# Scaling, transposing and splitting the state-space heads' output ahead of its projection, in another order

## The chip, the cores and the metric

The kernel runs on one core of a Trainium2 chip. The metric is the device time of one execution in microseconds (us). Each version was run several times; the median counts.

## What is computed

The reference is a chain of three transformer-like blocks on 256 tokens of width 1024. The change lies in the third, at the end of its state-space mixer. The 32 heads give y, 256 x 2048 values. With the gate z and eight groups of 256 columns:

```
y = y * silu(z)
y = y * rsqrt(mean(y^2 over each group of 256) + 1e-6) * norm_g
y_ssd = y @ w_ssd_o                    # 2048 x 1024
mixed = sigmoid(g_attn) * y_attn + sigmoid(g_ssd) * y_ssd
x = x + mixed @ w_out
```

All products are in f32 accuracy: the kernel makes one f32 product of three faster ones, from "upper" and "lower" halves of both operands (upper: the value rounded to fp32r, lower: the rest), as high x high + high x low + low x high.

## The kernel before

**Layout.** The 256 tokens are two tiles of 128 partitions (t = 0, 1; NT = 2). Every matrix product reads its weights from a stream of slots of 128 x 1024 values (512 KB), loaded by SyncE (L1530) into a ring of four buffers. A slot whose product is "split" gets its halves on the way: ScalarE copies the upper half to `wpair` (L477), and VectorE subtracts it from the raw slot for the lower one (L480). `wpair` has three places. The order of all this is written out by hand for each engine; there is no planner. The class Splitter keeps a counter of slots: `split.to(o)` splits all slots below o, `split.step()` the next one, `split.cover(stage)` all of a stage and up to two more. Both engines run through their own list in strict order, so a split stands exactly where it is written. Three counting semaphores tie it together: `w_hi` (upper half written), `w_lo` (lower half written; TensorE's `weights()` and SyncE's reload wait for it) and `w_used` (TensorE has used a slot up; ScalarE waits for slot o - 3 before it writes slot o). TensorE raises `w_used` with the first matmul or transpose behind the slot (`hold`, `release`).

**The stages here.** "gssd" (8 slots) is the product for the state-space gate g_ssd, "ssdo" (16 slots; slot k holds rows 128k to 128k + 127 of w_ssd_o) the projection of y, "wo3" the one by w_out. `ssdo_at` is the number of ssdo's first slot. The gate's first four slots give its lower 512 columns, before the heads; the last four ("gate pieces", L1858) lie beside the heads, two at their start and two behind them.

**The heads.** For each head TensorE sums rows (L1883, L1884), ScalarE takes exponentials (L2245, L2246), VectorE masks (L2895), and TensorE multiplies with x (L1897 to L1900). After each four heads VectorE adds (L2903) and multiplies with silu(z) (L2911), and ScalarE squares the group with a sum (L2236). At the end of the heads these run out one by one.

**Behind the heads, before the change.** VectorE splits one more slot, makes the mean squares (L2916, raises `y_ms`), ScalarE takes the square root (L2257; a load of its function table stands ahead of it), VectorE the reciprocal (L2919). Then VectorE scales y in four blocks of 512 columns: for both t a product with the reciprocal root (L2926), a wait, for both t a product with the row norm_g (L2930), a wait, and `y_normed` goes up by one (L2934). All four blocks are scaled before VectorE goes on. TensorE transposes y in eight groups of two 128-column blocks and both t (`y_group`, four transposes each, L1913), group i and i + 1 after block i / 2, into two PSUM banks in turn (6 and 7). ScalarE copies each group's upper half to `xpair` (L2272, raises `y_hi`), VectorE writes the lower half (L2941, raises `tr_out`). `xpair` holds four groups. TensorE waits with a bank for its lower half, two groups back. Groups 0 to 3 come ahead of ssdo's first product; groups 4 to 7 after slots 1, 3, 5 and 7. Group i serves slots 2i and 2i + 1. ssdo's result lies in banks 0 to 3. ScalarE and VectorE split up to slot 3 (`ssdo_at + 4`) ahead of their half of group 4, up to slot 5 ahead of group 5, and so on, and the rest behind group 7. ScalarE takes the two sigmoids of the gate (lower columns L2262, upper columns from the banks 0 and 1 L2265) ahead of its copies. On POOL, the load of the keys of a later stage (L1620) waits for the first `y_normed`. At the end VectorE gates the result and adds (L2949, L2952) and `mix3` is transposed for wo3 (L664).

Group 0 to 3 on TensorE, the last two lines being the order of the splits on ScalarE:

```
for i in range(4):
    y_group(i)
...
if k % 2 == 1 and k < 8:
    y_group(4 + k // 2)
...
if i >= 4:
    split.to(ssdo_at + 2 * (i - 4) + 4)
```

Of the kernel before, what the change touches and what calls it, by code (L numbers as in the profile page):

```python
# [27 lines left out]
ACT = mybir.ActivationFunctionType  # L28
AX = mybir.AxisListType

P = 128
# [353 lines left out]
def build(nc, wstream, rows, mixrow, cols, diag, consts, relb, keys, x_tok, xT_in, memT_in, ws, out, tbuf):  # L385
    ctx = ExitStack()
    with ctx:
# [5 lines left out]
        def S(name):  # L393

            if name not in sems:
                sems[name] = ctx.enter_context(nc.semaphore(name))
            return sems[name]
# [42 lines left out]
        def wait_lin(eng, g):  # L440

            if g > 0:
                for t in range(NT):
                    eng.wait_ge(S(f"lin_out{t}"), g)
# [74 lines left out]
        def bank(g, t):  # L519

            return psum[:, 2 * (g % 2) + t, :]
# [543 lines left out]
        def row_of(name):  # L1065
            return par[:, ROW[name] % 2, :]
# [360 lines left out]
        def y_pair(i, a):  # L1427

            return xpair[:, a, 2 * (i % 4):2 * (i % 4) + 2, :]

        def y_bank(i):
            return psum[:, 6 + (Q["y3"] + i) % 2, :].rearrange("p (c s) -> p c s", c=2)

        ssdo_at = ORDER[STAGES["ssdo"].slot][1]

# [199 lines left out]
        def _(pe):  # L1635
# [268 lines left out]

            def y_group(i):
                q = Q["y3"] + i
                if i % 2 == 0:
                    pe.wait_ge(S("y_normed"), i // 2 + 1)
                if q >= 2:
                    pe.wait_ge(S(f"tr_out{q % 2}"), q // 2)  # L1910
                for j in range(4):
                    c = 2 * i + j // 2
                    mm = pe.transpose(psum[:, 6 + q % 2, j * P:(j + 1) * P], y3[:, j % 2, c * P:(c + 1) * P], ident)  # L1913
                    if j == 0:
                        release(mm)
                mm.then_inc(S("tr_done"), 1)

            for i in range(4):
                y_group(i)
            s = STAGES["ssdo"]  # L1920
            wait_lin(pe, s.tile)
            for k in range(16):
                if k % 2 == 0:
                    q = Q["y3"] + k // 2
                    pe.wait_ge(S(f"tr_out{q % 2}"), q // 2 + 1)
                if k >= 14:
                    continue
                w = weights(pe, s.slot + k)
                for nn in range(2):
                    for t in range(NT):  # L1930
                        products(pe, bank(s.tile + nn, t), [xpair[:, a, k % 8, tt(t)] for a in (0, 1)],
                                 part(w, halves(nn)), k == 0, False)
                hold(s.slot + k)
                if k % 2 == 1 and k < 8:
                    y_group(4 + k // 2)
            w = [weights(pe, s.slot + k) for k in (14, 15)]
            for nn in range(2):
                for t in range(NT):
# [57 lines left out]
        def _(act):  # L1996
# [243 lines left out]
            for h in range(SSD_H):  # L2240
                act.wait_ge(S("rowsum"), h + 1)
                if h >= 4:
                    act.wait_ge(S("ydone"), h - 3)
                b = psum[:, 4 + h % 2, :]
                act.activation(ebuf[:, h % 4, 0:256], b[:, 0:256], ACT.Exp, bias=tiny[:, 12, h:h + 1])  # L2245
                act.activation(ebuf[:, h % 4, 256:384], b[:, 256:384], ACT.Exp, bias=tiny[:, 12, 32 + h:33 + h])\  # L2246
                   .then_inc(S("sexp"), 1)
                if h in (6, 7):
                    split.step()
                if h >= 10 and h % 4 in (2, 3):  # L2250
                    squares((h - 10) // 4, h % 4 - 2)
            for g in range((SSD_H - 10) // 4 + 1, SSD_G):
                for t in range(NT):
                    squares(g, t)
            split.step()
            act.wait_ge(S("y_ms"), 1)
            act.activation(grs, gst, ACT.Sqrt).then_inc(S("y_sd"), 1)  # L2257
            s = STAGES["gssd"]
            split.cover("gssd")
            act.wait_ge(S("lin_out0"), s.tile + 1)  # L2260
            act.wait_ge(S("lin_out1"), s.tile + 1)
            act.activation(g3[:, :, 0:HALF], g3[:, :, 0:HALF], ACT.Sigmoid).then_inc(S("gate3_low"), 1)  # L2262
            for t in range(NT):
                act.wait_ge(S(f"lin_done{t}"), s.tile + 2)
                act.activation(g3[:, t, HALF:D], bank(s.tile, t), ACT.Sigmoid).then_inc(S(f"lin_out{t}"), 1)  # L2265
            for i in range(8):
                if i >= 4:
                    split.to(ssdo_at + 2 * (i - 4) + 4)
                act.wait_ge(S("tr_done"), Q["y3"] + i + 1)
                if i >= 4:  # L2270
                    act.wait_ge(S("w_used"), ssdo_at + 2 * (i - 4) + 2)
                copy(y_pair(i, 0), y_bank(i)).then_inc(S("y_hi"), 1)  # L2272
            split.cover("ssdo", more=1)
            split.begin("wo3")
            act_x(act, "mix3")
# [62 lines left out]
        def _(dve):  # L2338
# [550 lines left out]
            for i in range(SSD_H + 5):  # L2889
# [16 lines left out]
                if h >= 0 and h % 4 == 3:  # L2906
                    g = h // 4
                    dve.wait_ge(S("yout"), g + 1)
                    for t in range(NT):
                        yg = y3[:, t, g * 256:(g + 1) * 256]  # L2910
                        dve.tensor_tensor(yg, yg, zz(t, g // 2)[:, g % 2 * 256:(g % 2 + 1) * 256], ALU.mult)\  # L2911
                           .then_inc(S("y_gated"), 1)
            split.step()

            dve.wait_ge(S("y_sq"), NT * SSD_G)
            chain(dve.tensor_scalar(gst, gst, 1.0 / 256, RMS_EPS, ALU.mult, ALU.add))  # L2916
            dve.nop().then_inc(S("y_ms"), 1)
            dve.wait_ge(S("y_sd"), 1)
            chain(dve.reciprocal(gst, grs))  # L2919
            wait_row(dve, "ssdn")  # L2920
            gate_end = ORDER[STAGES["gssd"].slot + STAGES["gssd"].nslot - 1][1] + 1
            for b in range(4):
                c = slice(b * HALF, (b + 1) * HALF)
                for t in range(NT):
                    yt = y3[:, t, c].rearrange("p (g d) -> p g d", g=2)
                    chain.mark(dve.tensor_tensor(yt, yt, gst[:, 8 * t + 2 * b:8 * t + 2 * b + 2].unsqueeze(2)  # L2926
                                                 .to_broadcast([P, 2, 256]), ALU.mult))
                chain.wait()
                for t in range(NT):
                    chain.mark(dve.tensor_tensor(y3[:, t, c], y3[:, t, c], row_of("ssdn")[:, c], ALU.mult))  # L2930
                    if split.at < gate_end:
                        split.step()
                chain.wait()
                dve.nop().then_inc(S("y_normed"), 1)  # L2934
            dve.nop().then_inc(S("row_used"), 1)
            split.cover("gssd")
            for i in range(8):
                if i >= 4:
                    split.to(ssdo_at + 2 * (i - 4) + 4)
                dve.wait_ge(S("y_hi"), i + 1)  # L2940
                dve.tensor_tensor(y_pair(i, 1), y_bank(i), y_pair(i, 0).bitcast(F32), ALU.subtract)\  # L2941
                   .then_inc(S(f"tr_out{(Q['y3'] + i) % 2}"), 1)
            split.cover("ssdo", more=1)
            s = STAGES["ssdo"]
            for n in range(2):
                for t in range(NT):
# [188 lines left out]
```

## Time and profile before

| what | value |
|---|---|
| time, median of 3 runs | 3109.84 us |
| lowest and highest | 3109.38, 3110.26 us |
| span of the profiled execution | 3107.9 us |
| the profiled execution's own time | not given apart from its span |
| mean granted clock of TensorE | 0.982 |
| busy TensorE / VectorE / ScalarE | 96% / 64% / 44% |
| instructions | 52456 |

The span runs from the first to the last instruction of one execution. A line such as L2941 is a line of the kernel. "Busy" of TensorE is the share of the span in which a matmul ran, by modelled ends. "Granted clock" is the share of 2.4 GHz that the chip lets TensorE have; its two levels are 1.00 (2.4 GHz) and 0.50 (1.2 GHz), and a mean over a stretch lies between them. A row of the timeline merges neighbours of the same kind: start in us, length in us from the start of the first to the end of the last, what, and in brackets the idle time of the engine before it, with what ended it.

### The profile page before, as it was taken

The page shows a single profiled execution, that of the slowest core. Times are in us where ns is not written, and L with a number is a line of the kernel's source. Part 1 is how long each engine was busy: PE and PEld are TensorE (multiplying, and loading weights), DVE is VectorE, ACT ScalarE, POOL GpSimd, SP SyncE. Part 2 cuts the span into 40 slices and gives each one's busy share as a digit, 9 for nine tenths or more (in the row PEclk, how much of TensorE's full clock was granted, in tenths as well). Part 3 has the DMA queues.
Part 4 walks back from the last instruction along what each step waited for, and adds up shares of the span by engine and source line. Part 5 has one row for each costly group of instructions (what it writes and reads, how often), then busy time and mean ns, then how long its engine had stood idle before and what let it go on. Part 6 is the DMA issues. An engine that isn't in the chain of part 4 may idle for free. (4 is left out here: it accounts for less than half of the span.)

```text
span 3107.9 us, 52456 instructions
## 1 busy us (share of the span) xinstructions
PE 2983.3 (96%) x19012; PEld 2654.8 (85%) x19012; DVE 1984.8 (64%) x3483; ACT 1362.0 (44%) x2015; POOL 197.6 (6%) x207
## 2 busy tenths in 40 slices
PE   8999998998999999999999999998898899999999
PEld 8987767997999699998799776997797888888888
DVE  5565565556557655556755664686599866666666
ACT  4333433434344334435343543565446744433333
POOL 0000000000000000000000000010057700000000
PEclk9999999999999999999999999999999999999999
DMA  7564253555554555555355543443442255555554
GB/s 275 188 216 150 102 176 129 190 187 202 184 185 154 189 188 183 185 187 183 131 199 186 186 156 118 163 143 103 142 157 89 69 188 189 184 187 179 179 183 159
DMA packets 140575, 523.73 MB, mean 169 GB/s; under 512 B 15698, under 2 KB 15698, under 8 KB 137616
## 3 DMA queue, kind: packets, MB, share of 16 engines
q1 hardware_dynamic: 135072, 490.79, 47.1%
q0 software_dynamic: 4784, 29.94, 2.6%
q8 instruction: 95, 1.56, 0.2%
q10 hardware_dynamic: 576, 1.05, 0.1%
q14 instruction: 48, 0.39, 0.0%
HBM read 520.65 MB, written 1.06 MB: 168 GB/s over the span
## 5 line engine op out<-in xcount | busy, mean ns | idle before, releaser
L480 DVE TENSOR_TENSOR wpair<-ring,wpair 128x1024 fp32r<-128x1024 f32 (+1 forms) x862 | 1044.5, 1220 | 740.2 <-ACT wpair L477 736.1
L509 PE MATMUL psum<-xpair,wpair 128*128 128x256 f32 x11712 | 1476.5, 285 | 21.3 <-DVE wpair L480 14.5
L509 PEld LDWEIGHTS psum<-xpair,wpair 128*128 128x128 f32 x11712 | 1444.5, 193 | 59.4 <-DVE wpair L480 35.1
L477 ACT CAST wpair<-ring 128x1024 fp32r<-128x1024 f32 (+1 forms) x888 | 919.0, 1044 | 815.5 <-PE psum L509 737.6
L509 PE MATMUL psum<-wpair,hpair 128*128 128x512 f32 x3120 | 751.6, 392 | 5.0 <-DVE hpair L942 5.0
L509 PEld LDWEIGHTS psum<-wpair,hpair 128*128 128x128 f32 x3120 | 572.7, 189 | 117.4 <-issue 7.5
L509 PE MATMUL psum<-wpair,xpair 128*128 128x512 f32 (+3 forms) x1728 | 403.2, 391 | 4.1 <-DVE wpair L480 1.8
L509 PEld LDWEIGHTS psum<-wpair,xpair 128*128 128x128 f32 x1728 | 321.9, 193 | 73.2 <-issue 7.2
L917 ACT ACTIVATE small<-psum 128x256 f32<-128x256 f32 x132 | 50.7, 384 | 230.9 <-PE psum L509 230.9
L953 ACT ACTIVATE small<-psum 128x256 f32<-128x256 f32 x92 | 35.4, 384 | 259.9 <-PE psum L509 259.9
L931 DVE TENSOR_TENSOR small<-small,psum 128x256 f32<-128x256 f32 x132 | 55.6, 421 | 136.7 <-ACT small L917 136.7
L1574 POOL DMA_DIRECT2D arena<-rows x18 | 9.6, 535 | 1533.3 <-DVEq L1127 1186.1
L942 DVE TENSOR_TENSOR hpair<-small,hpair 128x256 fp32r<-128x256 f32 x236 | 100.4, 426 | 8.1
L1984 PE MATMUL psum<-hpair,small 128*128 128x128 f32 x512 | 70.5, 281 | 12.3 <-ACT hpair L2317 10.2
L1984 PEld LDWEIGHTS psum<-hpair,small 128*128 128x128 f32 x512 | 63.2, 193 | 17.1 <-DVE small L3077 14.7
L3077 DVE TENSOR_SCALAR small<-kc,small 128x128 f32<-128x128 f32 x256 | 76.5, 341 | 0.1
L940 DVE CAST hpair<-small 128x256 fp32r<-128x256 f32 x236 | 69.4, 294 | 8.1
L480 POOL TENSOR_TENSOR wpair<-ring,wpair 128x1024 fp32r<-128x1024 f32 x26 | 62.5, 2409 | 163.5 <-DVE wpair L480 147.7
L722 ACT CAST xpair<-psum 128x512 fp32r<-128x512 f32 x60 | 34.2, 587 | 65.9 <-PE psum L664 39.7
L1005 DVE TENSOR_TENSOR small<-small,arena 128x256 f32<-128x256 f32 x92 | 60.9, 662 | 0.1
L1309 ACT ACTIVATE arena<-arena,st 128x128 f32<-128x128 f32 (+1 forms) x64 | 28.6, 447 | 73.8 <-DVE st L1339 73.8
L1230 DVE SCALAR_TENSOR_TENSOR arena<-arena,pcol 128x256 f32<-128x256 f32 x144 | 58.9, 480 | 1.1 <-DVE arena L2674 0.5
(344 smaller groups left out, 1813.3 us busy)
## 6 DMA issues: line engine op xcount, KB each, us to landing
ring<-wstream SPq DMA_DIRECT2D x934, 512.0 KB, 3.3
arena<-rows POOLq DMA_DIRECT2D x18, 1024.0 KB, 5.3
arena<-diag POOLq DMA_DIRECT2D x2, 1728.0 KB, 10.6
arena<-tbuf POOLq DMA_DIRECT2D x2, 1024.0 KB, 9.3
arena<-x_feat ACTq DMA_DIRECT2D x4, 256.0 KB, 7.4
res<-x_tok POOLq DMA_DIRECT2D x1, 1024.0 KB, 8.4
gb<-mem_feat POOLq DMA_DIRECT2D x1, 1024.0 KB, 17.4
arena<-keys POOLq DMA_DIRECT2D x1, 1024.0 KB, 5.2
```

What stands on the lines that cost most here:

```text
L477: eng.copy(hi, raw).then_inc(S("w_hi"), 1)
L480: eng.tensor_tensor(wpair[:, 1, o % PAIRS, 0:w], raw, hi.bitcast(F32), ALU.subtract)\
L509: mm = pe.matmul(out_, a[i], b[j], start=start and n == 0, stop=stop_ and last)
L917: act.activation(gated(f0 + f), psum[:, 4 + (f0 + f) % 2, 0:SEQ], ACT.Silu).then_inc(S("hid_act"), 1)
L931: dve.tensor_tensor(whole(h), gated(h), psum[:, 4 + h % 2, SEQ:2 * SEQ], ALU.mult)\
L940: dve.tensor_copy(hpair[:, 0, h % 2, :], src).then_inc(S("hid_hi"), 1)
L942: dve.tensor_tensor(hpair[:, 1, h % 2, :], src, hpair[:, 0, h % 2, :].bitcast(F32), ALU.subtract)\
L953: act.activation(gated(f), psum[:, 4 + f % 2, 0:SEQ], ACT.Gelu).then_inc(S("hid_act"), 1)
L1005: dve.tensor_tensor(whole(h), gated(f), weight(f + step * i), ALU.mult).then_inc(S("hid_whole"), 1)
L1230: chain.mark(eng.scalar_tensor_tensor(out=acc[:, f, :], in0=src, scalar=w, in1=acc[:, f, :], op0=ALU.mult, op1=ALU.add))
L1984: mm = pe.matmul(psum[:, n % 4, j * P:(j + 1) * P], oh1[:, n % 2, j, :], oh2[:, n % 2, j, :].bitcast(F32), start=True, stop=True)
L3077: ins = dve.tensor_scalar(oh1[:, n % 2, j, :], iota, selT[:, 0, tok], selT[:, 2, tok], ALU.is_equal, ALU.mult)
```

## The change

It touches only the end of the heads. Scalings go by groups of 256 columns in one fused pass for each t, and every pass raises `y_normed`. VectorE's list interleaves the scalings with splits and lower halves. Transposes use four banks (4 to 7) in turn; groups 0 and 1 come ahead of ssdo's slot 0, groups 2 and 3 behind it, and groups 4 to 7 behind slots 3, 5, 7 and 9. Slot 0 does the upper 512 columns first, so that it waits for the gate's banks later. ScalarE loads the table of the root ahead of the last squares and that of the sigmoid behind the root, and has the upper and lower gate sigmoids between and behind the first copies.

```diff
--- before.py
+++ after.py
@@ -1429,7 +1429,7 @@
             return xpair[:, a, 2 * (i % 4):2 * (i % 4) + 2, :]
 
         def y_bank(i):
-            return psum[:, 6 + (Q["y3"] + i) % 2, :].rearrange("p (c s) -> p c s", c=2)
+            return psum[:, 4 + i % 4, :].rearrange("p (c s) -> p c s", c=2)
 
         ssdo_at = ORDER[STAGES["ssdo"].slot][1]
 
@@ -1904,21 +1904,19 @@
 
             def y_group(i):
                 q = Q["y3"] + i
-                if i % 2 == 0:
-                    pe.wait_ge(S("y_normed"), i // 2 + 1)
-                if q >= 2:
-                    pe.wait_ge(S(f"tr_out{q % 2}"), q // 2)
+                pe.wait_ge(S("y_normed"), NT * (i + 1))
+                if i >= 4:
+                    pe.wait_ge(S(f"tr_out{q % 2}"), q // 2 - 1)
                 for j in range(4):
                     c = 2 * i + j // 2
-                    mm = pe.transpose(psum[:, 6 + q % 2, j * P:(j + 1) * P], y3[:, j % 2, c * P:(c + 1) * P], ident)
+                    mm = pe.transpose(psum[:, 4 + i % 4, j * P:(j + 1) * P], y3[:, j % 2, c * P:(c + 1) * P], ident)
                     if j == 0:
                         release(mm)
                 mm.then_inc(S("tr_done"), 1)
 
-            for i in range(4):
-                y_group(i)
+            y_group(0)
+            y_group(1)
             s = STAGES["ssdo"]
-            wait_lin(pe, s.tile)
             for k in range(16):
                 if k % 2 == 0:
                     q = Q["y3"] + k // 2
@@ -1926,13 +1924,18 @@
                 if k >= 14:
                     continue
                 w = weights(pe, s.slot + k)
-                for nn in range(2):
+                for nn in (1, 0) if k == 0 else (0, 1):
+                    if k == 0 and nn == 0:
+                        wait_lin(pe, s.tile)
                     for t in range(NT):
                         products(pe, bank(s.tile + nn, t), [xpair[:, a, k % 8, tt(t)] for a in (0, 1)],
                                  part(w, halves(nn)), k == 0, False)
                 hold(s.slot + k)
-                if k % 2 == 1 and k < 8:
-                    y_group(4 + k // 2)
+                if k == 0:
+                    y_group(2)
+                    y_group(3)
+                elif k % 2 == 1 and 3 <= k <= 9:
+                    y_group(4 + (k - 3) // 2)
             w = [weights(pe, s.slot + k) for k in (14, 15)]
             for nn in range(2):
                 for t in range(NT):
@@ -2249,27 +2252,39 @@
                     split.step()
                 if h >= 10 and h % 4 in (2, 3):
                     squares((h - 10) // 4, h % 4 - 2)
+            act.activation(spare, eps_col, ACT.Sqrt)
             for g in range((SSD_H - 10) // 4 + 1, SSD_G):
                 for t in range(NT):
                     squares(g, t)
-            split.step()
             act.wait_ge(S("y_ms"), 1)
             act.activation(grs, gst, ACT.Sqrt).then_inc(S("y_sd"), 1)
-            s = STAGES["gssd"]
-            split.cover("gssd")
-            act.wait_ge(S("lin_out0"), s.tile + 1)
-            act.wait_ge(S("lin_out1"), s.tile + 1)
-            act.activation(g3[:, :, 0:HALF], g3[:, :, 0:HALF], ACT.Sigmoid).then_inc(S("gate3_low"), 1)
-            for t in range(NT):
-                act.wait_ge(S(f"lin_done{t}"), s.tile + 2)
-                act.activation(g3[:, t, HALF:D], bank(s.tile, t), ACT.Sigmoid).then_inc(S(f"lin_out{t}"), 1)
-            for i in range(8):
-                if i >= 4:
-                    split.to(ssdo_at + 2 * (i - 4) + 4)
+            split.to(ssdo_at + 1)
+            act.activation(spare, eps_col, ACT.Sigmoid)
+            split.to(ssdo_at + 2)
+
+            def y_upper(i):
+
                 act.wait_ge(S("tr_done"), Q["y3"] + i + 1)
                 if i >= 4:
                     act.wait_ge(S("w_used"), ssdo_at + 2 * (i - 4) + 2)
                 copy(y_pair(i, 0), y_bank(i)).then_inc(S("y_hi"), 1)
+
+            s = STAGES["gssd"]
+            for t in range(NT):
+                act.wait_ge(S(f"lin_done{t}"), s.tile + 2)
+            y_upper(0)
+            y_upper(1)
+            for t in range(NT):
+                act.activation(g3[:, t, HALF:D], bank(s.tile, t), ACT.Sigmoid).then_inc(S(f"lin_out{t}"), 1)
+            split.to(ssdo_at + 3)
+            y_upper(2)
+            y_upper(3)
+            act.wait_ge(S("lin_out0"), s.tile + 1)
+            act.wait_ge(S("lin_out1"), s.tile + 1)
+            act.activation(g3[:, :, 0:HALF], g3[:, :, 0:HALF], ACT.Sigmoid).then_inc(S("gate3_low"), 1)
+            for i in range(4, 8):
+                split.to(ssdo_at + 2 * (i - 4) + 4)
+                y_upper(i)
             split.cover("ssdo", more=1)
             split.begin("wo3")
             act_x(act, "mix3")
@@ -2910,37 +2925,46 @@
                         yg = y3[:, t, g * 256:(g + 1) * 256]
                         dve.tensor_tensor(yg, yg, zz(t, g // 2)[:, g % 2 * 256:(g % 2 + 1) * 256], ALU.mult)\
                            .then_inc(S("y_gated"), 1)
-            split.step()
-
             dve.wait_ge(S("y_sq"), NT * SSD_G)
-            chain(dve.tensor_scalar(gst, gst, 1.0 / 256, RMS_EPS, ALU.mult, ALU.add))
-            dve.nop().then_inc(S("y_ms"), 1)
+            dve.tensor_scalar(gst, gst, 1.0 / 256, RMS_EPS, ALU.mult, ALU.add).then_inc(S("y_ms"), 1)
+            wait_row(dve, "ssdn")
             dve.wait_ge(S("y_sd"), 1)
             chain(dve.reciprocal(gst, grs))
-            wait_row(dve, "ssdn")
-            gate_end = ORDER[STAGES["gssd"].slot + STAGES["gssd"].nslot - 1][1] + 1
-            for b in range(4):
-                c = slice(b * HALF, (b + 1) * HALF)
+
+            def y_norm(g):
+
                 for t in range(NT):
-                    yt = y3[:, t, c].rearrange("p (g d) -> p g d", g=2)
-                    chain.mark(dve.tensor_tensor(yt, yt, gst[:, 8 * t + 2 * b:8 * t + 2 * b + 2].unsqueeze(2)
-                                                 .to_broadcast([P, 2, 256]), ALU.mult))
-                chain.wait()
-                for t in range(NT):
-                    chain.mark(dve.tensor_tensor(y3[:, t, c], y3[:, t, c], row_of("ssdn")[:, c], ALU.mult))
-                    if split.at < gate_end:
-                        split.step()
-                chain.wait()
-                dve.nop().then_inc(S("y_normed"), 1)
-            dve.nop().then_inc(S("row_used"), 1)
-            split.cover("gssd")
-            for i in range(8):
-                if i >= 4:
-                    split.to(ssdo_at + 2 * (i - 4) + 4)
+                    yg = y3[:, t, g * 256:(g + 1) * 256]
+                    dve.scalar_tensor_tensor(out=yg, in0=yg, scalar=gst[:, 8 * t + g:8 * t + g + 1],
+                                             in1=row_of("ssdn")[:, g * 256:(g + 1) * 256], op0=ALU.mult,
+                                             op1=ALU.mult).then_inc(S("y_normed"), 1)
+
+            def y_lower(i):
+
                 dve.wait_ge(S("y_hi"), i + 1)
                 dve.tensor_tensor(y_pair(i, 1), y_bank(i), y_pair(i, 0).bitcast(F32), ALU.subtract)\
                    .then_inc(S(f"tr_out{(Q['y3'] + i) % 2}"), 1)
+
+            y_norm(0)
+            y_norm(1)
+            split.to(ssdo_at + 1)
+            y_norm(2)
+            y_lower(0)
+            y_lower(1)
+            split.to(ssdo_at + 2)
+            y_norm(3)
+            split.to(ssdo_at + 3)
+            y_lower(2)
+            y_lower(3)
+            for g in range(4, SSD_G):
+                y_norm(g)
+            dve.wait_ge(S("y_normed"), NT * SSD_G)
+            dve.nop().then_inc(S("row_used"), 1)
+            for i in range(4, 8):
+                split.to(ssdo_at + 2 * (i - 4) + 4)
+                y_lower(i)
             split.cover("ssdo", more=1)
+            dve.wait_ge(S("gate3_low"), 1)
             s = STAGES["ssdo"]
             for n in range(2):
                 for t in range(NT):
```

## Rows read from the trace of the kernel before

**Rows 1.** The page: its first line.
```profile
span 3107.9 us, 52456 instructions
```

**Rows 2.** The chain that ended last, 2125 to 2200: start, length, what.
```profile
2132.78 1.31 DVE arena L2930 x2
...
2134.32 1.23 DVE wpair L480
```

**Rows 3.** TensorE's timeline, 2117 to 2200 us.
```profile
2117.91 5.73 PE L509 MATMUL psum<-wpair,xpair 128*128 128x512 f32 x24
2125.88 1.09 PE L1913 MATMUL psum<-kc,arena 128*128 128x128 f32 x8 [2.24 <-DVEq L2934]
2136.29 1.94 PE L1913 MATMUL psum<-kc,arena 128*128 128x128 f32 x8 [9.32 <-DVE xpair L2941]
2137.88 7.27 PE L509 MATMUL psum<-wpair,xpair 128*128 128x512 f32 x24
2144.99 0.60 PE L1913 MATMUL psum<-kc,arena 128*128 128x128 f32 x4
2145.35 5.74 PE L509 MATMUL psum<-wpair,xpair 128*128 128x512 f32 x24
...
2163.12 22.39 PE L509 MATMUL psum<-wpair,xpair 128*128 128x512 f32 x96
```

**Rows 4.** The timeline of all engines at the end of the heads, 2116 to 2127 us.
```profile
2116.71 0.21 ACT L2236 ACTIVATION_READ_ACCUMULATOR arena<-arena 128x1 f32 x1
...
2117.53 0.42 ACT L2236 ACTIVATE arena<-arena 128x256 f32<-128x256 f32 x1 [0.60 <-DVE arena L2911]
...
2118.86 0.76 DVE L2911 TENSOR_TENSOR arena<-arena 128x256 f32<-128x256 f32 x2
2119.32 0.42 ACT L2236 ACTIVATE arena<-arena 128x256 f32<-128x256 f32 x1 [0.88 <-DVE arena L2911]
...
2120.04 0.19 ACT L2236 ACTIVATION_READ_ACCUMULATOR arena<-arena 128x1 f32 x1
...
2121.19 1.28 ACT L2257 ACT_TABLE_LOAD   x1
...
2122.34 0.17 DVE L2916 TENSOR_SCALAR st<-st 128x16 f32<-128x16 f32 x1
...
2122.60 0.22 ACT L2257 ACTIVATE st<-st 128x16 f32<-128x16 f32 x1
...
2122.85 0.25 DVE L2919 RECIPROCAL st<-st 128x16 f32<-128x16 f32 x1 [0.34 <-ACT st L2257]
2123.14 1.29 DVE L2926 TENSOR_TENSOR arena<-arena,st 128x512 f32<-128x512 f32 x2
...
2126.04 1.06 ACT L2265 ACTIVATE arena<-psum 128x512 f32<-128x512 f32 x2
2126.12 0.64 POOL L1620 DMA_DIRECT2D arena<-keys  x1 [71.68 <-DVEq L2934]
```

**Rows 5.** VectorE's timeline, in the convolution before the heads.
```profile
2069.19 1.67 DVE L2870 SCALAR_TENSOR_TENSOR arena<-arena,pcol 128x256 f32<-128x256 f32 x4
```

**Rows 6.** The timeline of ScalarE and VectorE behind the transposes of group 4.
```profile
2145.63 0.59 ACT L2272 CAST xpair<-psum 128x512 fp32r<-128x512 f32 x1 [1.83 <-PE psum L1913]
2146.11 1.05 ACT L477 CAST wpair<-ring 128x1024 fp32r<-128x1024 f32 x1
...
2147.19 1.23 DVE L480 TENSOR_TENSOR wpair<-ring,wpair 128x1024 fp32r<-128x1024 f32 x1 [0.26 <-ACT wpair L477]
```

**Rows 7.** TensorE's timeline elsewhere: behind idle times of 1.39, 0.61 and 2.27 us.
```profile
1068.91 5.98 PE L509 MATMUL psum<-xpair,wpair 128*128 128x256 f32 x48 [1.39 <-DVE wpair L480]
...
2258.61 3.14 PE L509 MATMUL psum<-xpair,wpair 128*128 128x256 f32 x24 [0.61 <-DVE wpair L480]
...
2274.44 4.58 PE L509 MATMUL psum<-xpair,wpair 128*128 128x256 f32 x24 [2.27 <-DVE wpair L480]
```

**Rows 8.** Windows: stretch, its us, busy time (instructions) of each engine, clock, DMA, GB/s.
```profile
2274.00:2277.00 3.00, 2.56 (x12) 2.56 (x13) 2.96 (x17) 1.53 (x2) 2.52 (x2) 0.55 0.47 147
```

## The prediction

> **What bounds the kernel now.** I first read the page and then three views of the stretch between the last state-space head and the output product ("ssdo"). TensorE carries the kernel, so this change can move the time only where TensorE stands still. [Rows 1] give the span against which the sum is made. In the chain of waits, look for which engine holds the chain while TensorE is idle: it is VectorE, with the last of the scalings (L2926, L2930) and one split of weights (L480) [rows 2]. TensorE's own timeline shows the two gaps: 2.24 us before the first eight transposes, and 9.32 us before the next eight, which VectorE's first lower halves (L2941) end [rows 3]. The first product of ssdo starts at 2137.88. TensorE had finished the gate pieces at 2117.91 + 5.73 = 2123.64. So 14.2 us lie between them, of which 3 are transposes. From 2137.88 on TensorE is hardly ever idle until 2185.51 (2163.12 + 22.39), and all splits run in its shadow. Two prices follow. One slot is 12 matmuls: 22.39 less a tail of 0.15, over 8, is 2.78 us. One group of transposes adds 2145.35 - 2144.99 = 0.36 us [rows 3]. I first ask what starts the products earlier, then whether the shadow behind them still holds.
>
> **Before the first product.**
> (1) The wait for the root. The last square ends at 2120.23; the split of slot 0 and a table load of 1.28 us stand between it and the root [rows 4]. After the change the table comes ahead of the squares: ScalarE is free at 2116.92, load and a small activation of 0.2 us last to 2118.4, two squares of group 6 to 2119.25, and group 7 is ready at 2119.32 as before. The 0.60 us and 0.88 us that ScalarE idled there [rows 4] hide the load; without them it would cost up to 1.28. VectorE's split before the mean square also goes. Mean square at 2120.3 (0.17), root (0.22), reciprocal (0.25), with small gaps: the first scaling starts at 2121.05 in place of 2123.14.
> (2) The scalings. Sixteen passes of 512 at about 0.65 (two in 1.29, [rows 4]) become sixteen fused ones of 256. Not seen in this form; the nearest row is the convolution's, four of 128x256 in 1.67 with one of them about 0.48, so 0.40 us apart [rows 5]. Bounds are 0.34 (two plain products of that size take 0.75, [rows 4]) and 0.50. Groups 0 and 1 end at 2122.7, the split of slot 0 (1.14 apart) at 2123.8, group 2 at 2124.6.
> (3) The transposes. Group 0 starts when the gate pieces end, 2123.64, and is out 0.60 later, 2124.25. ScalarE after the root: slot 0 (1.0), load of the sigmoid table (1.28), small activation (0.2), slot 1 (1.0), so also 2124.25. Upper half 0.59, lower half 0.69, 0.13 to TensorE: **the first product starts at 2125.7, which is 12.2 us earlier.** Only 1.0 us of idle time is left.
> At this place a rule speaks against the change. The table loads here last 1.28 us and the next instruction starts right behind (2121.19 + 1.28 = 2122.47, and the root, which also waits for VectorE, runs at 2122.60) [rows 4]. The Trainium skill, "ScalarE: Activation LUTs", section "What ACT_TABLE_LOAD costs", adds a drain of about 1380 ns, 2.66 us a switch; the loads' gaps in this trace do not show it. What it would do is a rival below.
> (4) Clock. The first 24 matmuls of ssdo take 7.27 us, the next 24 take 5.74 [rows 3]: they started at 1.2 GHz after the 9.32 us gap. With a gap of 1.0 this goes: **-1.5 us**.
> (5) Groups 2 and 3 of the transposes now stand behind slot 0: two times 0.36, **+0.7 us**. The upper gate's sigmoid (two in 1.06, [rows 4]) ends at 2126.3, before the second half of slot 0 needs its banks at 2127.1: nothing. The lower gate's sigmoid (1.06) comes in ScalarE's wait for group 4: nothing; its reader on VectorE comes at the end of ssdo. The load of the keys on POOL's queue starts at some 2121.5 in place of 2126.12 [rows 4], runs 1 MB beside SP's loads, and nobody waits for it before the next stage but one. SP's loads follow VectorE's splits: that for slot 4 is issued at 2123.9 in place of 2122.6 and wanted after 2138: nothing.
> (6) VectorE's queue. In order: low 0 and 1 to 2126.1, split 1 to 2127.2, group 3 to 2128.0, split 2 to 2129.2, low 2 and 3 from 2129.7 (they wait for group 2 and 3, transposed at 2128.5) to 2130.9, groups 4 to 7 (8 times 0.40) to 2134.2, and only then split 3, to 2135.6. TensorE wants slot 3 at 2134.8. **+0.9 us**, from 0.4 to 1.7 by the bounds in (2). If this is late it is the only early stop.
>
> **Behind the first product.** Here the cover is lost. Group i of the last four is now transposed after slots 3, 5, 7, 9, but the splits are still written as "to slot 4 for group 4, to 6 for group 5, ..." on ScalarE and VectorE, each ahead of that group's halves. When TensorE reaches slot 4, ScalarE has cast slots 0 to 3 and stands in its wait for group 4, which TensorE has only just transposed. The cast of slot 4 is queued behind the copy of group 4, VectorE's split behind its lower half. The same holds for slots 6, 8 and 10. Before the change group 4 came after slot 1 with slots 2 and 3 already split, so 5.6 us of products hid this chain. Its length stands in one round of the trace: transposes start at 2144.99, copy at 2145.63, cast at 2146.11, VectorE's split from 2147.19 to 2148.42 [rows 6]. With 0.13 to TensorE that is 3.56 us after the start of the group, where TensorE would have gone on after 0.36: 3.2 us a stop. The bounds are 2.8 and 3.7. **Four stops, +12.8 us.**
> Sum so far: -12.2 - 1.5 + 0.7 + 0.9 + 12.8 = **+0.7 us**.
> (7) Clock at the stops. TensorE will be idle for some 3.0 us four times. Rows of before bound what that costs. After 1.39 us of idle time 48 matmuls took 5.98, or 24 in 2.99: nothing. After 2.27 us 24 of the same shape took 4.58, against 3.14 a little earlier: 1.4 us [rows 7], and the granted clock of those 3 us was 0.55 [rows 8]. After 9.32 us: 1.5 on products and 0.85 on transposes (1.94 against 1.09, [rows 3]), some 2. The 2.27 us row is the nearest. I take 1.3 a stop, a little less, since the clock may fall while TensorE still waits: **+5.2 us**, from 0 to 8.
> Behind ssdo the same steps follow in the same order, later by the shift: 0, plus or minus 1.5, since the low stretches there can fall otherwise.
> Total +5.9 us on a profiled span of 3107.9, so a span of 3113.8. The runs' median stands 1.9 above that span, and the shift is the same: 3109.84 + 5.9 = **3115.7 us**. A measurement of this kernel can tell about 0.2%, 6.2 us, from no change. The forecast is thus no change that can be told, at the slow edge: 12 us won and given back.
>
> **Rivals.**
> A, slower by more than 0.2%. The place is the first products behind each of the four stops. The forecast's clock price is 1.3 a stop; from (6.2 - 0.7) / 4 = 1.37 on the change counts as slower. For it: the stops are longer than the 2.27 us gap that cost 1.4, and the long gap cost about 2. Against: one low stretch may begin within the stop. At 2.0 a stop: 0.7 + 8.0 = +8.7, 3118.5 us. Chance 0.38.
> B, the clock doesn't fall, as after 1.39 us of idle time [rows 7]: +0.7, 3110.5 us. Against it stands the 2.27 us row. 0.08.
> C, faster: the stops don't occur, the splits being ahead after all, or being much shorter than 3.2. Then -12.1, 3097.7 us. For it: in before, casts do run two slots ahead. Against: the order of the queues, as written. 0.05.
> D, a table switch costs ScalarE more than its row. With 1.4 us more on each of the two moved loads the last square ends 1.1 later and the first upper half 2.4 later; TensorE ends 2.4 later: +8.3, 3118.1 us. Against: no gap behind a load in [rows 4]. 0.05. The rule of "ScalarE: Activation LUTs" named above would be this case.
> The forecast has the rest, 0.44.
>
> **How the numbers follow.** Within 0.2%: forecast and B, 0.52. Slower: A and D, 0.43. Faster: C, 0.05. The range leaves out C and the upper part of A and D: 3110 to 3119 us.
>
> **What would show it.** In the changed profile: first product of ssdo near 2125.7 with under 1.5 us idle before it; its first 24 matmuls without the 7.27; four idle times of TensorE of about 3.0 us, released by VectorE's split (L480), each behind four transposes, at slots 4, 6, 8 and 10; ScalarE waiting some 6 to 7 us for TensorE's transposes each time; granted clock under 1.00 behind the stops; last product of ssdo at about 2191 in place of 2185.5. The forecast is wrong if TensorE runs through at slot 4, or if the stops are there and the granted clock stays at 1.00.

## The result, and the profile after

The changed kernel takes 3118.79 us in the median of six runs (3112.62 to 3126.03), the kernel before 3110.05 us beside it (six runs, 3109.22 to 3117.47). The ratio is 1.0022 with a 95% interval from 1.0011 to 1.0032: slower by about 0.2%, which is where the prediction drew its line. It lies inside the range (3110 to 3119 us). The profiled execution took 3116.99 us with a span of 3115.1 us, 7.2 us longer than before.

TensorE's timeline of the changed kernel, from the last two gate pieces to the transposes of mix3 (start, length, what, and in brackets the idle time before it and what ended it), answers to [rows 3]:

```profile
2118.32 5.74 PE L509 MATMUL psum<-wpair,xpair 128*128 128x512 f32 x24
2123.90 1.03 PE L1912 MATMUL psum<-kc,arena 128*128 128x128 f32 x8
2125.97 3.03 PE L509 MATMUL psum<-wpair,xpair 128*128 128x512 f32 x12 [1.04 <-DVE xpair L2945]
2128.84 1.04 PE L1912 MATMUL psum<-kc,arena 128*128 128x128 f32 x8
2129.63 5.73 PE L509 MATMUL psum<-wpair,xpair 128*128 128x512 f32 x24
2135.97 3.02 PE L509 MATMUL psum<-wpair,xpair 128*128 128x512 f32 x12 [0.61 <-DVE wpair L480]
2138.84 0.60 PE L1912 MATMUL psum<-kc,arena 128*128 128x128 f32 x4
2142.41 8.50 PE L509 MATMUL psum<-wpair,xpair 128*128 128x512 f32 x24 [2.97 <-DVE wpair L480]
2150.74 0.60 PE L1912 MATMUL psum<-kc,arena 128*128 128x128 f32 x4
2154.31 7.35 PE L509 MATMUL psum<-wpair,xpair 128*128 128x512 f32 x24 [2.97 <-DVE wpair L480]
2161.50 0.60 PE L1912 MATMUL psum<-kc,arena 128*128 128x128 f32 x4
2165.07 7.31 PE L509 MATMUL psum<-wpair,xpair 128*128 128x512 f32 x24 [2.97 <-DVE wpair L480]
2172.22 0.60 PE L1912 MATMUL psum<-kc,arena 128*128 128x128 f32 x4
2175.79 18.48 PE L509 MATMUL psum<-wpair,xpair 128*128 128x512 f32 x72 [2.97 <-DVE wpair L480]
2194.30 1.09 PE L664 MATMUL psum<-kc,arena 128*128 128x128 f32 x8
```

Read it in two halves. The 9.32 us of idle time of [rows 3] has become 1.04, and the first product starts at 2125.97. Then four idle times of 2.97 us have appeared, each behind four transposes and each ended by VectorE's split of weights; and behind three of them 24 matmuls take 7.3 to 8.5 us that took 5.74 elsewhere, behind the fourth 72 take 18.48. ScalarE and VectorE at the first of the four, from the timeline of all engines, answer to [rows 6]:

```profile
2139.47 0.58 ACT L2270 CAST xpair<-psum 128x512 fp32r<-128x512 f32 x1 [7.03 <-PE psum L1912]
2139.95 1.99 ACT L477 CAST wpair<-ring 128x1024 fp32r<-128x1024 f32 x2
2140.09 0.69 DVE L2945 TENSOR_TENSOR xpair<-psum,xpair 128x512 fp32r<-128x512 f32 x1 [4.17 <-ACT xpair L2270]
2141.03 2.36 DVE L480 TENSOR_TENSOR wpair<-ring,wpair 128x1024 fp32r<-128x1024 f32 x2 [0.26 <-ACT wpair L477]
```

ScalarE waited 7.03 us for TensorE's transposes, doing nothing, and only then could cast the weights that TensorE wanted at once. At the other three stops it waited 9.43, 8.28 and 8.24 us. The windows of the changed kernel (stretch, its us, busy time and instructions of PE, PEld, DVE, ACT, POOL, granted clock, DMA share, GB/s) show the clock behind the first two stops:

```profile
2136.00:2140.00 4.00, 3.44 (x16) 2.64 (x16) 0.00 (x0) 0.53 (x2) 0.00 (x0) 1.00 0.43 133
2140.00:2144.00 4.00, 1.59 (x4) 1.34 (x5) 3.05 (x3) 1.95 (x3) 0.00 (x0) 0.70 0.16 34
2144.00:2148.00 4.00, 4.00 (x11) 3.14 (x10) 0.00 (x0) 0.00 (x0) 0.00 (x0) 0.50 0.73 235
2148.00:2152.00 4.00, 3.34 (x16) 2.52 (x14) 0.01 (x1) 0.62 (x2) 0.00 (x0) 0.95 0.00 0
...
2156.00:2160.00 4.00, 4.00 (x14) 3.19 (x13) 0.00 (x0) 0.00 (x0) 0.00 (x0) 0.67 0.68 223
```

From 2144 to 2148 eleven matmuls ran at 0.50, that is 1.2 GHz.

Since the start of this stretch moves from run to run for reasons that lie upstream (last section), the experiments are compared by a measure of their own, **the stretch**: from the start of the last gate pieces to the start of mix3's transposes (L664). It is 2185.55 - 2117.91 = 67.6 us before the change and 2194.30 - 2118.32 = 76.0 with it, so 8.3 us more. The distance from the gate pieces to the first product of ssdo is 19.97 us before the change and 7.65 us with it.

### The profile page after: what moved, and what is told of

Same layout as the page of the kernel before. It is cut to its first block and busy times, and to the rows that moved or that the text cites. A ratio compares the mean times of both kernels' runs of the same rounds, so it can differ in the third digit from the quotient of the medians.

```text
span 3115.1 us, 52455 instructions
## 1 busy us (share of the span) xinstructions
PE 2988.3 (96%) x19012; PEld 2657.5 (85%) x19012; DVE 1980.1 (64%) x3483; ACT 1361.6 (44%) x2017; POOL 197.5 (6%) x207
## 5 line engine op out<-in xcount | busy, mean ns | idle before, releaser
L509 PE MATMUL psum<-wpair,xpair 128*128 128x512 f32 (+3 forms) x1728 | 412.0, 397 | 17.4 <-DVE wpair L480 14.0
L931 DVE TENSOR_TENSOR small<-small,psum 128x256 f32<-128x256 f32 x132 | 55.6, 421 | 136.9 <-ACT small L917 136.9
L1987 PE MATMUL psum<-hpair,small 128*128 128x128 f32 x512 | 71.3, 283 | 12.3 <-ACT hpair L2332 10.2
```

Source lines behind the costliest of these rows:

```text
L509: mm = pe.matmul(out_, a[i], b[j], start=start and n == 0, stop=stop_ and last)
L931: dve.tensor_tensor(whole(h), gated(h), psum[:, 4 + h % 2, SEQ:2 * SEQ], ALU.mult)\
L1987: mm = pe.matmul(psum[:, n % 4, j * P:(j + 1) * P], oh1[:, n % 2, j, :], oh2[:, n % 2, j, :].bitcast(F32), start=True, stop=True)
```

## The experiments

Theory: the early part of the change wins some 12 us, and the move of groups 4 to 7 loses more, because it puts the splits of slots 4, 6, 8 and 10 behind transposes that TensorE makes just ahead of these slots.

**Splits two slots ahead.** The changed kernel with, on ScalarE and on VectorE:

```diff
-                split.to(ssdo_at + 2 * (i - 4) + 4)
+                split.to(ssdo_at + 2 * (i - 4) + 6)
```

> The changed kernel, but ScalarE and VectorE split two slots further ahead of each of groups 4 to 7 (to slot 6, 8, 10, 12 in place of 4, 6, 8, 10). Theory (the cast of slots 4, 6, 8, 10 is queued behind a group that TensorE has only just transposed): all four idle times of 2.97 us go, and with them the low clock behind them. In the changed kernel's trace the four stops cost 4 x 3.2 on length and 7.6 on clock, so the last product of ssdo ends at about 2174 instead of 2194.3, and the time is 20 us under the changed kernel's profiled 3117.0: about 3097 us, 13 us under the kernel before. Rival (the cast waits for a free place in wpair, that is for TensorE to use a slot up, and the place in the queue is beside the point): the stops stay, some 3 us each, and the time stays at 3117.

Measured: 3100.55 us in the median of seven runs, ratio to the kernel before 0.9965 (0.9953 to 0.9978). The stretch is 55.6 us, 20.3 less than with the change. TensorE's timeline of this kernel:

```profile
2139.86 3.06 PE L509 MATMUL psum<-wpair,xpair 128*128 128x512 f32 x12 [0.61 <-DVE wpair L480]
2142.76 0.60 PE L1912 MATMUL psum<-kc,arena 128*128 128x128 f32 x4
2143.12 5.74 PE L509 MATMUL psum<-wpair,xpair 128*128 128x512 f32 x24
2148.70 0.60 PE L1912 MATMUL psum<-kc,arena 128*128 128x128 f32 x4
2149.05 5.72 PE L509 MATMUL psum<-wpair,xpair 128*128 128x512 f32 x24
```

No idle time stands behind the transposes, and every pair of slots takes 5.7 us. `wpair` still has three places, so the rival falls. The median is 3.5 us above the 3097 expected; the stretch came out as expected. In the profiled execution (3101.74 us) the gate pieces started 3.9 us later than in the changed kernel's, and the part behind the stretch took 1.2 us longer; what set these two was not tried.

**Groups 4 to 7 where they were.** The changed kernel with, on TensorE:

```diff
-                elif k % 2 == 1 and 3 <= k <= 9:
-                    y_group(4 + (k - 3) // 2)
+                elif k % 2 == 1 and k <= 7:
+                    y_group(4 + k // 2)
```

> The changed kernel, but TensorE transposes groups 4 to 7 behind slots 1, 3, 5, 7, as before the change, and the splits stay as the change has them. Theory of the queue order: the same as with the splits further ahead, no stops at slots 4, 6, 8, 10, about 3097 us; at most 1 us more, since group 4's scaling ends at about 2132, when slot 1 ends too. Rival (wpair's places bind): about 3117 us. A second rival (VectorE's scaling of group 4 is late for slot 1, so TensorE waits there): 3098 to 3100 us with one idle time ahead of group 4.

Measured: 3098.44 us, ratio 0.9962 (0.9948 to 0.9977), stretch 55.2 us. The same gain from the other side of the same misfit: it is the distance between a group's place on TensorE and the splits' place on the other two engines that counts. VectorE is not late for group 4.

**One part alone: the groups late in the kernel before.**

```diff
-                if k % 2 == 1 and k < 8:
-                    y_group(4 + k // 2)
+                if k % 2 == 1 and 3 <= k <= 9:
+                    y_group(4 + (k - 3) // 2)
```

> The kernel before, with one part of the change alone: groups 4 to 7 are transposed behind slots 3, 5, 7, 9 instead of 1, 3, 5, 7, with the splits as they were. Theory: four stops of 3.2 us plus 1.9 us of clock each appear, +20 us: about 3130 us against 3110. If the clock takes only the 1.3 us a stop that the prediction had: +18 us, 3128. Rival (the stops need the new order of VectorE's list too, or wpair's places bind): no stops, 3110 us.

Measured: 3130.78 us, ratio 1.0063 (1.005 to 1.0077); stretch 87.3 us, 19.6 more than before. The four stops are there, with nothing else of the change:

```profile
2149.63 0.60 PE L1913 MATMUL psum<-kc,arena 128*128 128x128 f32 x4
2153.20 7.34 PE L509 MATMUL psum<-wpair,xpair 128*128 128x512 f32 x24 [2.97 <-DVE wpair L480]
2160.38 0.60 PE L1913 MATMUL psum<-kc,arena 128*128 128x128 f32 x4
2163.95 7.32 PE L509 MATMUL psum<-wpair,xpair 128*128 128x512 f32 x24 [2.97 <-DVE wpair L480]
```

So this one step of the change makes the four stops by itself. The clock took 1.6 us at each of them here: the matmuls behind three of them took 7.34, 7.32 and 7.33 us in place of 5.74, and the last 72 took 18.50 in place of the 16.93 of the kernel with the splits ahead. That lies between the 1.3 and the 1.9 of the expectation, and the median can't tell 18 us from 20.

**What the clock takes at a stop.** The changed kernel with spare products behind each of groups 4 to 7, into a bank that nobody reads:

```diff
                 elif k % 2 == 1 and 3 <= k <= 9:
                     y_group(4 + (k - 3) // 2)
+                    for _ in range(14):
+                        pe.matmul(psum[:, 4 + ((k - 3) // 2 + 1) % 4, 0:384], ident_r, segs, start=True, stop=True)
```

> The changed kernel with 14 spare matmuls of 384 columns behind each of groups 4 to 7, into a bank that nobody reads; they do nothing but keep TensorE running for some 2.3 of the 3.0 us. Theory (a stop costs 3.2 us of length, and 1.9 us more because the granted clock falls): the four stops keep their length, slots 4, 6, 8, 10 start 3.57 us behind their group's transposes as they do now, but the granted clock stays 1.00 and the pairs of slots behind them take 5.74 us instead of 7.3 to 8.5: 7 to 8 us less than the changed kernel, about 3109.5 us, the same as before the change. Rival (the slower products behind the stops come from something else, such as VectorE or ScalarE crossing their operands): no change, 3117 us.

Measured: the stretch is 68.4 us, 7.5 less than with the change; 3113.96 us in the median of twelve runs, ratio to before 1.0009 (1.0001 to 1.0018). Its timeline:

```profile
2148.11 0.60 PE L1912 MATMUL psum<-kc,arena 128*128 128x128 f32 x4
2148.46 2.70 PE L1940 MATMUL psum<-hpair 128*128 128x384 f32 x14
2151.68 5.71 PE L509 MATMUL psum<-wpair,xpair 128*128 128x512 f32 x24 [0.52 <-DVE wpair L480]
```

Slot 4 starts 2151.68 - 2148.11 = 3.57 us behind the start of the group, exactly as in the changed kernel (2142.41 - 2138.84 = 3.57): the stop is as long. But with TensorE kept busy the next 24 matmuls take 5.71 us, and the windows give a granted clock of 1.00:

```profile
2152.00:2156.00 4.00, 4.00 (x19) 3.31 (x18) 0.67 (x1) 0.00 (x0) 0.00 (x0) 1.00 0.74 241
```

So a stop costs 3.2 us of length, and the clock took 7.5 us at the four, 1.9 on average; the clock's part is shown apart from the rest. Against the kernel with the splits ahead the stretch is 68.4 - 55.6 = 12.8 us longer, which is the length of four stops alone. The clock's 7.5 us are not spread evenly: 8.50 - 5.74 = 2.8 at the first stop, 1.6 at each of the others. What makes the first one dearer was not tried. The stretch came as expected. The median fell by 4.8 us, not by 7 to 8; this profiled execution reached the gate pieces at 2127.57 us, 9 us later than the changed kernel's.

**What the early part owes to each of its parts.** Four kernels follow, each run once, each with one part undone in the kernel with the splits two slots ahead (7.65 us to the first product, stretch 55.6). A single time says little here, so the four are read by their stretch.

The root's table behind the squares again:

```diff
-            act.activation(spare, eps_col, ACT.Sqrt)
             for g in range((SSD_H - 10) // 4 + 1, SSD_G):
```

> The kernel with the splits two slots ahead (the first experiment), but without the early load of the root's table: the load stands behind the last squares again. Measured on the stretch from the start of the last two gate pieces to the start of mix3's transposes (55.6 us with the splits ahead, 67.6 before the change, 76.0 with it). Theory: the load of 1.28 us ends 1.3 after the last square, where the root had waited 0.4 for the mean square anyway, so root, reciprocal and the first product come 0.6 to 0.9 later: first product 8.3 to 8.5 us behind the start of the gate pieces in place of 7.65, stretch 56.3. Rival (the early load hides nothing, since transposes or the sigmoid's table bind): no change, 7.65 and 55.6.

Measured: first product at 8.50, as expected, but stretch 58.1 us, 2.4 more. The timeline and the windows show where the other 1.6 went:

```profile
2131.03 4.62 PE L509 MATMUL psum<-wpair,xpair 128*128 128x512 f32 x12 [1.87 <-DVE xpair L2944]
```

```profile
2131.00:2134.00 3.00, 2.97 (x8) 2.35 (x9) 3.00 (x5) 1.66 (x3) 0.00 (x0) 0.59 0.89 336
```

An idle time of 1.87 us behind eight transposes was enough: 12 matmuls took 4.62 us in place of 3.03, at a granted clock of 0.59. Behind the 1.04 us of the first experiment's kernel they took 3.02. I had expected a stretch of 56.3, so this one is a miss, by the clock.

The lower halves behind all scalings:

```diff
-            y_lower(0)
-            y_lower(1)
...
-            y_lower(2)
-            y_lower(3)
             for g in range(4, SSD_G):
                 y_norm(g)
+            for i in range(4):
+                y_lower(i)
```

> The kernel with the splits two slots ahead, but VectorE writes the lower halves of groups 0 to 3 behind all eight scalings, as before the change; scalings stay fused. Theory (the gap before the first product was VectorE's list, not the amount of scaling): first product 14 to 15 us behind the start of the gate pieces in place of 7.65, that is about 7 later; the idle time of some 8 us in front of it lowers the clock again, 1.5 to 2 us; slot 3's wait of 0.6 goes; stretch 63 to 64.5 us. Rival (the fusing made the gain, the order of the lower halves none): 1 us later at most, stretch under 57.

Measured: first product at 14.37, stretch 63.0 us, 7.4 more.

```profile
2136.78 4.59 PE L509 MATMUL psum<-wpair,xpair 128*128 128x512 f32 x12 [7.75 <-DVE xpair L2945]
```

The order of VectorE's list is a large part of the gain: undone, it costs 6.7 of the 12.3 us before the first product, and 1.6 of clock. The wait at slot 3 is gone here, as expected.

Each scaling in two passes:

```diff
-                    dve.scalar_tensor_tensor(out=yg, in0=yg, scalar=..., in1=..., op0=ALU.mult, op1=ALU.mult)
+                    chain.mark(dve.tensor_tensor(yg, yg, gst[...].to_broadcast([P, 256]), ALU.mult))
+                chain.wait()
...
+                    dve.tensor_tensor(yg, yg, row_of("ssdn")[...], ALU.mult)
```

> The kernel with the splits two slots ahead, but each group is scaled in two passes (by the root, a wait, by the row) instead of the fused one; order and all else stay. Theory: some 0.65 us more a group. First product about 1.9 later than 7.65 (three groups stand ahead of it on VectorE): 9.5; slot 3's split, behind all eight groups, 5.2 later, so TensorE waits some 3.9 us there in place of 0.6, with 1.5 us of clock: stretch 55.6 + 1.9 + 3.3 + 1.5 = 62.3, between 60 and 63. Rival (fusing is hidden by the waits for the halves): under 57.

Measured: first product at 9.45, and 3.31 us of idle time at slot 3 in place of 0.61; stretch 63.3 us, 7.7 more. Both idle times bring the clock down (12 matmuls in 4.29 and in 4.61). That is 0.3 us over the upper end expected: I had put clock at slot 3 alone, and the 2.55 us ahead of slot 0 brought it down too.

```profile
2132.06 4.29 PE L509 MATMUL psum<-wpair,xpair 128*128 128x512 f32 x12 [2.55 <-DVE xpair L2949]
...
2146.36 4.61 PE L509 MATMUL psum<-wpair,xpair 128*128 128x512 f32 x12 [3.31 <-DVE wpair L480]
```

Two banks for the transposes:

```diff
-                if i >= 4:
-                    pe.wait_ge(S(f"tr_out{q % 2}"), q // 2 - 1)
+                if i >= 2:
+                    pe.wait_ge(S(f"tr_out{q % 2}"), q // 2)
...
-                    mm = pe.transpose(psum[:, 4 + i % 4, j * P:(j + 1) * P], ...)
+                    mm = pe.transpose(psum[:, 6 + q % 2, j * P:(j + 1) * P], ...)
```

> The kernel with the splits two slots ahead, but the transposes use two banks in turn, as before the change, with the wait for the lower half two groups back. Theory: with groups 2 and 3 behind slot 0, lower halves 0 and 1 are written before TensorE gets there, so two banks do as well: first product 7.65, stretch 55.6, within 0.2. Rival (the four banks carry part of the gain): an idle time ahead of group 2 or 3, stretch 56.5 or more.

Measured: 7.65 and 55.6 us, the same. The four banks are worth nothing in this order. The other three, undone one by one, cost 0.85, 6.72 and 1.80 us at the first product, together 9.4 of 12.3 us. The rest of the change (groups 2 and 3 behind slot 0, slot 0's upper columns first, VectorE's split and ScalarE's sigmoids moved out of the way) was not undone alone, so what each of these is worth is not shown.

**A better version.** The kernel with the splits two slots ahead, and on VectorE:

```diff
             for g in range(4, SSD_G):
+                if g == 6:
+                    split.to(ssdo_at + 4)
                 y_norm(g)
```

> The kernel with the splits two slots ahead, and VectorE's split of slot 3 ahead of the scaling of groups 6 and 7, not behind it. Theory (the 0.61 us of idle time at slot 3 is VectorE's scaling of the last four groups): it goes, nothing else moves: stretch from the gate pieces to mix3's transposes 55.0 in place of 55.6, time about 0.6 us under the first experiment's, too little for the medians to tell: 3097 to 3100. Rival (the cast of slot 3 on ScalarE, behind the lower gate's sigmoid, binds as well): some 0.3 us or more of idle time stays at slot 3.

Measured: 3097.67 us in the median of six runs, ratio to the kernel before 0.9952 (0.9939 to 0.9965): 0.5% faster than before the change. The medians can't tell it from the first experiment's. The stretch is 54.7 us, 0.9 less than there; 0.6 was expected. Slots 1, 2 and 3 run through:

```profile
2130.78 8.45 PE L509 MATMUL psum<-wpair,xpair 128*128 128x512 f32 x36
```

The only idle time that the timeline still lists between the gate pieces and mix3 is the 1.04 us in front of slot 0.

## Why the prediction was right, and where it was not

**The early start** (the steps up to the first product). Predicted 12.2 us earlier, measured 19.97 - 7.65 = 12.3. The clock there came as predicted too: slot 0's 12 matmuls take 3.03 us, as slot 3's do (3.02), so the 1.5 us that the 9.32 us of idle time had cost are gone. The root's table hides beside the squares as worked out; undone, it costs 0.85 and the clock. VectorE's fused scaling was priced at 0.40 us apart from the nearest row; the changed kernel's timeline gives four in 1.68 with one of them 0.48:

```profile
2121.48 1.68 DVE L2938 SCALAR_TENSOR_TENSOR arena<-arena,st 128x256 f32<-128x256 f32 x4
...
2131.30 3.25 DVE L2938 SCALAR_TENSOR_TENSOR arena<-arena,st 128x256 f32<-128x256 f32 x8
```

**The table loads.** ScalarE's timeline shows both moved loads at 1.28 us with the next instruction right behind, so rival D is out:

```profile
2117.36 1.28 ACT L2255 ACT_TABLE_LOAD   x1
2118.65 0.20 ACT L2255 ACTIVATE st<-st 128x1 f32<-128x1 f32 x1
...
2122.06 1.28 ACT L2262 ACT_TABLE_LOAD   x1
2123.35 0.20 ACT L2262 ACTIVATE st<-st 128x1 f32<-128x1 f32 x1
```

The Trainium skill, "ScalarE: Activation LUTs", section "What ACT_TABLE_LOAD costs", adds a drain of about 1380 ns to every switch to another table set. This trace does not show it: 2117.36 + 1.28 = 2118.64, and the next instruction starts at 2118.65.

**Slot 3** was predicted to wait 0.9 us for VectorE, and waits 0.61. Moving one split took it away, so the cause was the one named.

**The stops.** Predicted four, at slots 4, 6, 8 and 10, each 3.56 us from the start of a group to the next product; measured four, 3.57. That the loss comes from the place of the groups against the splits is shown three ways: by moving the splits, by moving the groups, and by moving the groups alone in the kernel before. Rival C (no stops) is out, and so is B (the clock stays), by the 0.50 in the windows above. ScalarE's waits were to be 6 to 7 us and were 7.03 to 9.43; the three longer ones stand behind the slow products.

**The clock at the stops**, step (7), is the term that was mis-sized. I took 1.3 us a stop from the row behind 2.27 us of idle time (1.4), and took something off because the clock might fall while TensorE still waits. (The upper bound was read a little low: 1.5 on products and 0.85 on transposes are 2.35, not some 2.) Measured: 8.50 - 5.74, 7.35 - 5.74, 7.31 - 5.74, and 18.48 - 16.93 for the last 72 (16.93 is the same row with the splits ahead), together 7.5 us or 1.9 a stop against 5.2 and 1.3. The spare products give 7.5 too, but from the same profile of the changed kernel: they show that it is the clock, and don't measure its price a second time. Three of the four stops cost 1.6, as all four do with the late groups alone, and the first one 2.8. The discount failed where it should have held: in the wait of the first stop the granted clock was already down (0.88 from 2139.3 to 2142.3 us, 1.00 in the second stop's wait), and that stop cost most. On this term rival A (from 1.37 up, 2.0 a stop, 3118.5 us) is what happened, on average. Whether the whole change is slower by more than 0.2%, as A has it, is not settled: the interval of the ratio is 0.11% to 0.32%. Step for step the stretch was to grow by 5.9 us and grew by 8.3; 2.3 of the 2.4 us between them are this term.

**Behind ssdo** I had put 0, plus or minus 1.5. In the profiled executions of all eleven kernels the part from mix3's transposes to the end took between 919.9 and 922.8 us (before 922.35, after 920.80). So the 1.6 us by which this part was shorter after the change are within what differs from kernel to kernel there. They took back much of the clock's 2.3 us: the span grew by 8.3 - 1.6 + 0.4 (the gate pieces' later start) = 7.2 us, against 5.9.

**Luck.** The median, 3118.79 us, lies 0.2 us inside the upper end of the range and 0.3 from rival A's 3118.5. The six runs lie between 3112.62 and 3126.03, so both are chance. What the runs bear out is the mechanism: the early gain, the four stops, where they stand and how long they are.

## What to carry to other kernels

When two engines prepare operands in hand-written order, a step moved on the engine that uses them must be checked against every queue that waits for it: whatever is written behind that wait is late too, and here it was the weights of the very next slot. While the splits ran two slots ahead, a chain of 3.2 us stayed hidden at no cost. With the groups moved by two slots and the splits left where they were, it cost 5.1 us each time (4.9 in the kernel before), and a change that wins 12 us looked like a loss. When a large rework comes out near zero, look for idle times that repeat, and undo their one line before giving the rest up.

## What was not expected of the hardware

An idle time of under 2 us can cost the clock. Behind eight transposes 1.04 us of idle time cost nothing (12 matmuls in 3.03), 1.87 us cost 1.6 (4.62); 1.39 us between large products cost nothing [rows 7]. Whether the transposes have a part in it is not shown. Nor does the price follow the length of the idle time in these traces: 1.87 us cost the products behind it 1.6 us, 2.97 us cost them 1.6 in seven of eight stops and 2.8 in one, 7.75 us cost them 1.6.

The same code ahead of the change does not take the same time in each execution. The gate pieces start at 2114.57 us in the kernel with two banks, at 2117.91 before the change, at 2127.57 in the kernel with spare products, 13 us between the first and the last of these, whose code ahead of the heads' end is the same. A part of it can be seen in the heads. The windows of the kernel before, and then of the kernel with spare products:

```profile
2098.00:2102.00 4.00, 4.00 (x34) 3.95 (x33) 2.88 (x7) 3.12 (x11) 0.00 (x0) 1.00 0.02 4
```

```profile
2098.00:2102.00 4.00, 4.00 (x19) 3.90 (x17) 1.22 (x3) 1.28 (x4) 0.00 (x0) 0.50 0.00 0
```

In one execution the chip grants 1.2 GHz in the middle of the heads, with 19 matmuls in 4 us, in another 2.4 GHz with 34, while the longest idle time of TensorE in the 30 us before is 0.54 us in both. What decides it was not tried. Its consequence is that a change of a few microseconds is better read from a stretch of the trace than from the medians: the stretch came out within 0.1 us of 55.6 in two kernels whose spans were 3099.9 and 3092.6 us. A stretch with stops in it is less sure, as the 1.6 and 2.8 us above show.
